# Index block: the sample tile first, its scores with the cached keys between the prompt's score steps, single PSUM banks

## The chip, the cores and the metric

The kernel runs on one core of a Trainium2 chip. The metric is the device time of one launch in microseconds (us); lower is better. Engines are TensorE (PE), VectorE (DVE), ScalarE (ACT), GpSimd (POOL) and the DMA queues that SyncE (SP) and POOL issue to.

## What is computed

The program is one inference step of a two-layer decoder for a prompt of 1024 tokens and a sample group of 8 x 8 = 64 tokens. The part that is changed is the lightning indexer at the start of each layer: it scores keys for each query, and the best 256 are kept later.

```
z = x @ w_in_l
qi = rope(a_qi.reshape(B, L, IDX_HEADS, IDX_DIM), pos) * (IDX_DIM ** -0.5)
ki = rope(a_ki[:, :, None, :], pos)[:, :, 0, :]
wi = a_w * (IDX_HEADS ** -0.5)
def index_scores(qi, ki, wi):
    dots = jnp.einsum('bthd,bsd->bths', qi.astype(F32), ki.astype(F32))
    return jnp.einsum('bth,bths->bts', wi.astype(F32), jax.nn.relu(dots))
```

A prompt query is scored with the prompt's keys up to itself. A sample query is scored with 2048 cached keys of its own batch entry, gathered through a page table, and with the 8 new keys. There are 8 heads of 32. Everything is in f32.

## The kernel before

Each of the two layers runs a chain of blocks; between two blocks all engines meet. The first is `index_block` (line 406), the second `mixer_block`, whose DVE begins at once with the top-k search (`find`, lines 318 and 322) over the scores that `index_block` left, and whose PE begins at once with the input projections (line 889).

`index_block` works on nine tiles of tokens: 0 to 7 are 128 prompt rows each, 8 is the 64 sample rows. Its parts, on each engine in program order:

- **Transposed input.** PE turns all nine tiles (line 478) and ACT and DVE copy them to SBUF.
- **Per tile t:** PE multiplies the tile by the index columns of the weights (line 523, eight matmuls of 296 columns, the "input group" below). ACT copies the result (lines 602, 603). DVE applies the rotary embedding (lines 680 to 689, "rope"). PE turns the roped rows (`turn`, line 489), one tile later, and ACT copies them (`qk`, line 581). The input group has two PSUM banks in turn (4 and 5), the turned rows two (6 and 7).
- **Score steps** (`score_steps`, line 394). Prompt tiles 2 to 7 have 2, 2, 4, 4, 4 and 4 steps: a step is 256 to 512 keys by four of the eight heads. PE makes four row-packed matmuls into four banks (`score`, line 508), ACT takes the relu of all four (`relu`, line 592, "score relu") into one of two buffers `r`, and DVE adds the heads up with their weights (`add`, lines 660 and 662). The steps of tile t-2 stand in the program behind the input group of tile t. The sample tile's own keys are one more step (`own_step`, line 512), just ahead of tile 7's four. Up to it all steps use banks 0 to 3; tile 7's alternate between banks 0 to 3 and 4 to 7.
- **Sample scores with the cached keys**, after all steps: eight pairs of matmuls (`sample_score`, line 550: two row tiles of 64 rows, 512 keys, into two banks), one relu over both (line 617), and two matmuls that sum over heads (`sample_sum`, line 559), with a last copy to the score tile `S` (line 619). They need the sample's queries spread out by DVE (16 copies, line 706) and the weights turned (lines 692, 535, 610).

POOL gathers the cached keys by 32 indirect DMAs (line 627) from the block's start; SP writes the block's input rows out (lines 452, 453), since `r` takes their place, and loads the mixer's first weights (line 462) when the last input group is done. Semaphores in the code order everything: `s_sr` counts score relus, `s_sp` score steps on PE, `s_zs`, `s_zr`, `s_zd` the sample's scores, relus and sums.

Of the kernel before, what the change touches and what calls it, by code (L numbers as in the profile page):

```python
# [31 lines left out]
P = 128  # L32
# [373 lines left out]


def index_block(e):
# [19 lines left out]
    own_step = next(n for n, x in enumerate(steps) if x[0] == NT - 1)  # L428
    of_tile = lambda t: [n for n, x in enumerate(steps) if x[0] == t]
    set_of = lambda n: (n - own_step) % 2 if n > own_step else 0  # L430
    added = [4 * (n + 1) + (4 if n >= own_step else 0) for n in range(len(steps))]
# [13 lines left out]
    with nc.Block() as block:  # L445
# [23 lines left out]
        def _(pe):  # L469

            for t in range(NT):
                R = rows(t)
                for half in range(2):
                    g = 2 * t + half
# [8 lines left out]
            def turn(t):  # L483
                R = rows(t)
                pe.wait_ge(s_ro, t + 1)
                if t >= 2:
                    pe.wait_ge(s_qk, t - 1)
                for n, src in enumerate((rr[0:R, t % 2, 0:128], rr[0:R, t % 2, 128:256], kr[0:R, t % 2, :])):
                    ins = pe.transpose(bank(6 + t % 2)[:, n * P:n * P + R], src, ident[0:R, 0:R])
                ins.then_inc(s_qp, 1)  # L490

            def score(n):
                t, _, a, b, g = steps[n]
                pe.wait_ge(s_qk, t + 1)
# [3 lines left out]
                if n == own_step + 1:  # L498
                    pe.wait_ge(s_zi, NT)
                    pe.wait_ge(s_qk, NT)  # L500
                    pe.wait_ge(s_ws, 1)
                before = [m for m in range(n) if set_of(m) == set_of(n)]
                if before:
                    pe.wait_ge(s_sr, before[-1] + 1)
                for h in range(4):
                    part, out = slice(32 * h, 32 * h + 32), bank(4 * set_of(n) + h)
# [9 lines left out]
            for t in range(NT):  # L516
                R = rows(t)
                pe.wait_ge(s_ta, t + 1)
                pe.wait_ge(s_td, t + 1)
                if t >= 2:  # L520
# [5 lines left out]
                if t:  # L526
                    turn(t - 1)
                for n in of_tile(t - 2):
                    score(n)
            turn(NT - 1)  # L530

            pe.wait_ge(s_wd, 1)
            pe.wait_ge(s_zi, NT - 1)
            for pair in range(4):
                ins = pe.transpose(bank(5)[:, pair * NS:(pair + 1) * NS], WD[0:NS, pair * P:(pair + 1) * P],
                                   ident[0:NS, 0:NS])
            ins.then_inc(s_wt, 1)
            for n in range(own_step, len(steps)):
                score(n)

            def sample_score(n):
                a, g = n // 2, n % 2
                if n == 0:
                    pe.wait_ge(s_qb, 1)
                    pe.wait_ge(s_kit, layer * (16 * 2 * NPG) + 16 * 2 * NPG)
                if n >= 2:
                    pe.wait_ge(s_zr, n - 1)
                for rr_ in range(2):
                    part = slice(64 * rr_, 64 * rr_ + 64)
                    ins = pe.matmul(bank(2 * (n % 2) + rr_), QB[part, g, :], kitc[part, g, 512 * a:512 * a + 512],  # L550
                                    start=True, stop=True)
                ins.then_inc(s_zs, 1)

            def sample_sum(n):
                a, g = n // 2, n % 2
                pe.wait_ge(s_zr, n + 1)
                for rr_ in range(2):
                    half = a // 2
                    ins = pe.matmul(bank(4 + a % 2)[64 * half:64 * half + 64, :], WS[:, 2 * g + rr_, :],
                                    rs[:, n % 2, 512 * rr_:512 * rr_ + 512],  # L560
                                    start=(g == 0 and rr_ == 0), stop=(g == 1 and rr_ == 1))
                ins.then_inc(s_zd, 1)

            pe.wait_ge(s_sr, len(steps))
            sample_score(0)
            for n in range(8):
                if n < 7:
                    sample_score(n + 1)
                sample_sum(n)

        @block.scalar
        def _(act):
            ch = chains(e, act, "act")
            for t in range(NT):
                act.wait_ge(s_tp, 2 * t + 1)
                act.copy(XT[:, 0:4, tcol(t)], bank((2 * t) % 4).rearrange("p (c n) -> p c n", c=4)[:, :, 0:rows(t)]
                         ).then_inc(s_ta, 1)

            def qk(t):
                act.wait_ge(s_qp, t + 1)  # L580
                act.copy(QKI[:, :, tcol(t)], bank(6 + t % 2, 384).rearrange("p (c n) -> p c n", c=3)[:, :, 0:rows(t)]
                         ).then_inc(s_qk, 1)

            def relu(n):
# [5 lines left out]
                if n >= 2:  # L590
                    act.wait_ge(s_sd, added[n - 2])
                act.activation(r[0:R, n % 2, 0:4 * w].rearrange("p (h s) -> p h s", h=4),
                               ps[0:R, 2048 * set_of(n):2048 * set_of(n) + 2048].rearrange(
                                   "p (h s) -> p h s", h=4)[:, :, 0:w], ACT.Relu).then_inc(s_sr, 1)

            for t in range(NT):
                R = rows(t)
                act.wait_ge(s_zp, t + 1)
                if t >= 2:
                    act.wait_ge(s_ro, t - 1)  # L600

                act.mul(w_idx[0:R, t, :], bank(4 + t % 2, 296)[0:R, 288:296], (ID * IH) ** -0.5)
                act.copy(zi[0:R, t % 2, 0:288], bank(4 + t % 2, 296)[0:R, 0:288]).then_inc(s_zi, 1)
                if t:
                    qk(t - 1)
                for n in of_tile(t - 2):
                    relu(n)
            qk(NT - 1)
            act.wait_ge(s_wt, 1)
            act.copy(WS.rearrange("p a s -> p (a s)"), bank(5, 4 * NS)).then_inc(s_ws, 1)  # L610
            for n in range(own_step, len(steps)):
                relu(n)
            for n in range(8):
                act.wait_ge(s_zs, n + 1)
                if n >= 2:
                    act.wait_ge(s_zd, n - 1)
                act.activation(rs[:, n % 2, :], ps[:, 1024 * (n % 2):1024 * (n % 2) + 1024], ACT.Relu).then_inc(s_zr, 1)
            act.wait_ge(s_zd, 8)
            act.copy(S[:, SOFF:SOFF + HALF], ps[:, 2048:3072]).then_inc(s_ss, 1)
# [2034 lines left out]
```

## Time and profile before

| | |
|---|---|
| time, median of 3 runs | 4244.15 us (4241.81 to 4248.46) |
| profiled execution: its time / its span | 4248.55 us / 4246.7 us |
| busy: PE, DVE, ACT, POOL | 3840.8 (90%), 2057.7 (48%), 978.3 (23%), 1171.1 (28%) |
| mean granted TensorE clock | 0.924 of 2.4 GHz |

The shares of the whole span tell little here: the program is a chain of blocks with different limits. The block that the change touches is read in stretches of its own, once per layer: from 25.8 to 163.6 us in the first and from 2129.7 to 2270.1 us in the second. In the profile an f32 matmul leaves two records, so x8 on PE is four matmuls.

### The profile page before, as it was taken

The numbers are of one execution on the slowest core, as the hardware profiler recorded it, in microseconds if no ns is written. First come the engines' busy times: TensorE is split into PE (matmuls) and PEld (weight loads), VectorE is DVE, ScalarE is ACT, GpSimd is POOL, SyncE is SP. The second block draws the span as 40 slices with busy tenths as digits, with TensorE's granted clock in tenths as the row PEclk, the third lists the DMA queues.
The fourth block names the chain that finished last, engine by engine and source line by source line (L and its number), as shares of the span: only waits on it lengthen the run. The fifth ranks groups of instructions, "written<-read, shape, count | busy, mean of one in ns | idle before, by whom it ended". The sixth has DMA issues, their size and how long they took to land. (4 is left out here: it accounts for less than half of the span.)

```text
span 4246.7 us, 50144 instructions
## 1 busy us (share of the span) xinstructions
PE 3840.8 (90%) x18986; PEld 2644.4 (62%) x18986; DVE 2057.7 (48%) x4149; ACT 978.3 (23%) x1930; POOL 1171.1 (28%) x1043
## 2 busy tenths in 40 slices
PE   6899977889897999999879999878898989999996
PEld 4344564444466988889643445644445578889985
DVE  5799564533044333333667994555221443333335
ACT  3201134420132221112231012344211221111222
POOL 3014672313023112122330155622130322122113
PEclk9899957989998999999979999579899989999998
DMA  3111002460211111111020110034602121111101
GB/s 141 41 44 39 14 1 86 160 220 21 79 40 60 49 50 40 40 40 43 6 96 26 41 45 6 1 135 149 202 0 80 40 80 40 40 40 40 56 33 42
DMA packets 143022, 254.97 MB, mean 60 GB/s; under 512 B 24577, under 2 KB 76162, under 8 KB 142594
## 3 DMA queue, kind: packets, MB, share of 16 engines
q1 hardware_dynamic: 130562, 215.00, 14.8%
q0 software_dynamic: 12288, 37.76, 2.6%
q8 instruction: 98, 1.61, 0.2%
q14 instruction: 74, 0.61, 0.0%
HBM read 231.31 MB, written 21.42 MB: 60 GB/s over the span
## 5 line engine op out<-in xcount | busy, mean ns | idle before, releaser
L2403 PE MATMUL ps<-ffn_parts 128*128 128x512 f32 (+1 forms) x3456 | 801.7, 391 | 7.4 <-DVE arena L2533 7.4
L2393 PE MATMUL ps<-ffn_parts 128*128 128x384 f32 (+1 forms) x4608 | 778.6, 329 | 23.0 <-POOL ffn_parts L2478 23.0
L2393 PEld LDWEIGHTS ps<-ffn_parts 128*128 128x128 f32 x4608 | 774.3, 189 | 28.2 <-POOL ffn_parts L2478 23.9
L2403 PEld LDWEIGHTS ps<-ffn_parts 128*128 128x128 f32 (+1 forms) x3456 | 623.4, 182 | 174.7 <-DVE arena L2533 24.3
L2533 DVE TENSOR_TENSOR arena<-arena,ps 128x1024 f32<-128x1024 f32 (+1 forms) x288 | 351.2, 1219 | 342.3 <-PE ps L2403 338.2
L889 PE MATMUL ps<-arena,arena_rest 128*128 128x512 f32 (+1 forms) x1152 | 379.5, 492 | 3.7 <-PEq L445 2.7
L2483 POOL TENSOR_TENSOR ffn_parts<-arena,ffn_parts 128x1024 fp32r<-128x1024 f32 x64 | 153.9, 2404 | 607.5 <-ACT ffn_parts L2437 607.5
L899 PE MATMUL ps<-arena_rest,arena 128*128 128x512 f32 (+3 forms) x864 | 318.7, 526 | 2.3 <-ACT arena_rest L1072 2.3
L889 PEld LDWEIGHTS ps<-arena,arena_rest 128*128 128x128 f32 x1152 | 191.7, 193 | 193.5 <-issue 192.1
L322 DVE TENSOR_SCALAR_CACHE_REDUCE arena_rest<-arena_rest,small 128x384 bf16<-128x384 f32 (+4 forms) x330 | 278.8, 875 | 2.1
L1941 PE MATMUL ps<-arena_rest,arena 128*128 128x512 f32 (+1 forms) x576 | 256.0, 604 | 20.7 <-DMA arena_rest<-in_w_out 20.7
L2525 DVE TENSOR_TENSOR arena<-arena 128x384 f32<-128x384 f32 (+1 forms) x96 | 77.1, 828 | 363.8 <-ACT arena L2456 363.8
L899 PEld LDWEIGHTS ps<-arena_rest,arena 128*128 128x128 f32 (+1 forms) x864 | 157.7, 185 | 142.3 <-issue 130.9
L1865 POOL TENSOR_TENSOR arena<-arena,arena_rest 128x1024 f32<-128x1024 f32 (+1 forms) x34 | 79.7, 2345 | 493.3 <-DVE arena L1857 493.3
L2437 ACT CAST ffn_parts<-arena 128x1024 fp32r<-128x1024 f32 x64 | 67.1, 1049 | 640.6 <-PE ps L2403 618.3
L1502 POOL DMA_INDIRECT arena_rest<-in_kv,kv_rows x128 | 135.4, 1058 | 277.4 <-PE ps L1616 239.7
L1941 PEld LDWEIGHTS ps<-arena_rest,arena 128*128 128x128 f32 (+1 forms) x576 | 106.9, 188 | 159.8 <-issue 137.1
L318 DVE TENSOR_SCALAR_CACHE_REDUCE arena_rest<-arena_rest,small 128x1088 bf16<-128x1088 f32 (+1 forms) x132 | 168.0, 1310 | 2.4
L949 PE MATMUL ps<-arena_rest 64*128 64x64 f32 (+2 forms) x1088 | 127.6, 405 | 45.4 <-POOLq L1263 23.7
L2478 POOL TENSOR_TENSOR ffn_parts<-arena,ffn_parts 128x512 fp32r<-128x512 f32 x64 | 82.2, 1295 | 305.9 <-ACT ffn_parts L2434 305.9
L2525 DVE TENSOR_TENSOR ffn_raw<-ffn_raw 128x384 f32<-128x384 f32 (+1 forms) x96 | 48.4, 532 | 241.9 <-ACT ffn_raw L2456 241.9
L2478 POOL TENSOR_TENSOR ffn_parts<-ffn_raw,ffn_parts 128x512 fp32r<-128x512 f32 x64 | 84.7, 1334 | 280.0 <-ACT ffn_parts L2434 280.0
(299 smaller groups left out, 4951.4 us busy)
## 6 DMA issues: line engine op xcount, KB each, us to landing
arena_rest<-in_kv SPq DMA_DIRECT2D x128, 256.0 KB
arena<-in_w_down SPq DMA_DIRECT2D x32, 1024.0 KB, 7.6
arena_rest<-in_w_in SPq DMA_DIRECT2D x10, 2048.0 KB, 8.1
ffn_raw<-in_w_up SPq DMA_DIRECT2D x16, 1024.0 KB, 5.9
arena<-in_w_up SPq DMA_DIRECT2D x16, 1024.0 KB, 5.9
out_y_prompt<-arena SPq DMA_DIRECT2D x3, 4096.0 KB, 15.9
arena<-out_y_prompt SPq DMA_DIRECT2D x2, 4096.0 KB, 24.8
arena_rest<-in_mem_kT SPq DMA_DIRECT2D x16, 512.0 KB, 7.1
```

What stands on the lines that cost most here:

```text
L318: ch.mark(dve.tensor_scalar(M16[:, moff:moff + w], S[:, off:off + w], thr[:, i:i + 1], None, op, ALU.add, accum_out=cnt[:, i:i + 1]))
L322: ch.mark(dve.tensor_scalar(M16[:, moff:moff + w], S[:, off:off + w], thr[:, i:i + 1], None, op, ALU.add, accum_out=cnt[:, i:i + 1]))
L889: ins = pe.matmul(ps[:, (f % 2) * 1536 + a:(f % 2) * 1536 + b], buf[:, k, c * P:(c + 1) * P], XT[:, k, a:b], start=(k == 0), stop=(k == KC ...
L899: ins = pe.matmul(bank(6 + u % 2, w)[0:R, :], XT[:, k, tcol(t)], buf[:, k, c0:c0 + w], start=(k == 0), stop=(k == KC - 1))
L949: ins = pe.matmul(second(ps[0:R, a:a + R], m), lhs[part, c, cols], second(rhs[part, c, cols], m), start=True, stop=True)
L1502: pool.indirect_dma_start(KV[b % 2][1][:, pg, :], None, i["kv"].rearrange("n p w -> (n p) w"), bass.IndirectOffsetOnAxis(ap=e["kvrow"][:, ...
L1941: ins = pe.matmul(bank(2 * (t % 2) + a)[0:R, :], YT[:, k, tcol(t)], WO[:, k, 512 * a:512 * a + 512], start=(k == 0), stop=(k == KC - 1))
L2393: ins = pe.matmul(bank(3 * c + b, y - x), w[:, k, :], h[:, k, x:y], start=(k == 0 and h is HH and w is WH), stop=(k == KC - 1 and w is WL))
L2403: ins = pe.matmul(bank(b0 + a)[0:R, :], u[:, c, tcol(t)], d[:, c, 512 * a:512 * a + 512], start=(c == 0 and u is UH and d is DH), stop=(c ...
L2478: pool.tensor_tensor(WL[:, ks, :], WU[n][:, ks, c * P:(c + 1) * P], WH[:, ks, :], ALU.subtract).then_inc(s_uh, 1)
L2483: pool.tensor_tensor(DL[:, c, :], WD[:, c, :], DH[:, c, :], ALU.subtract).then_inc(s_dl, 1)
L2533: dve.tensor_tensor(X[0:R, t, :], X[0:R, t, :], ps[0:R, b0:b0 + 1024], ALU.add).then_inc(s_ad, 1)
```

## The change

1. **The sample tile comes first.** `TILES` puts tile 8 ahead of tiles 0 to 7 in every loop; `j` is the place in that order. Its own-key step is step 0, the turning of its weights (DVE, PE, ACT) stands at place 1, the 16 spreading copies and the own-key adds on DVE at place 2.
2. **The cached-key scores are cut in 16 units** (one matmul of 64 rows by 512 keys, one relu, one summing matmul), all through bank 7, and stand behind score steps 9 to 20: on PE `score(n)`, then the sum of the unit before and the score of this one; on ACT the score relu of step n, then the unit's. Steps 14, 16 and 18 carry two units, and the last unit stands behind all steps. Sums gather in bank 6, and ACT copies each finished half out (`summed`).
3. **Single banks elsewhere:** the input group has bank 4 alone, turned rows bank 5, all score steps banks 0 to 3.

```diff
 def score_steps():
-    steps = []
+    steps = [(NT - 1, 0, 0, 2 * NS, 0)]
     for t, off, w in score_jobs():
-        if t == NT - 2:
-            steps.append((NT - 1, 0, 0, 2 * NS, 0))
...
-    set_of = lambda n: (n - own_step) % 2 if n > own_step else 0
+    TILES = [NT - 1] + list(range(NT - 1))
+    UNITS = [(a, g, rr_) for a in (0, 2, 1, 3) for g in range(2) for rr_ in range(2)]
+    units_behind, u = {n: [] for n in range(len(steps))}, 0
+    for n in range(9, len(steps)):
+        k = 2 if n in (14, 16, 18) else 1
+        units_behind[n] = list(range(u, u + k))
+        u += k
+    units_last = list(range(u, len(UNITS)))
...
             def score(n):
-                before = [m for m in range(n) if set_of(m) == set_of(n)]
-                if before:
-                    pe.wait_ge(s_sr, before[-1] + 1)
+                else:
+                    pe.wait_ge(s_sr, n)
...
+            def sample_score(u):
+                a, g, rr_ = UNITS[u]
+                if u == 0:
+                    pe.wait_ge(s_qb, 1)
+                    pe.wait_ge(s_kit, layer * (16 * 2 * NPG) + 16 * 2 * NPG)
+                else:
+                    pe.wait_ge(s_zr, u)
+                part = slice(64 * rr_, 64 * rr_ + 64)
+                pe.matmul(bank(7), QB[part, g, :], kitc[part, g, 512 * a:512 * a + 512],
+                          start=True, stop=True).then_inc(s_zs, 1)
+            def sample_sum(u):
+                pe.wait_ge(s_zr, u + 1)
...
+                pe.matmul(bank(6)[half:half + 64, :], WS[:, 2 * g + rr_, :], rs[:, u // 2 % 2, 512 * rr_:512 * rr_ + 512],
+                          start=(u % 4 == 0), stop=(u % 4 == 3), skip_group_check=True).then_inc(s_zd, 1)
+            def sample(u):
+                if u:
+                    sample_sum(u - 1)
+                sample_score(u)
...
-                if t >= 2:
-                    pe.wait_ge(s_zi, t - 1)
+                if j:
+                    pe.wait_ge(s_zi, j)
                 for k in range(KC):
-                    ins = pe.matmul(bank(4 + t % 2, 296)[0:R, :], XT[:, k, tcol(t)], wb[:, k, :],
+                    ins = pe.matmul(bank(4, 296)[0:R, :], XT[:, k, tcol(t)], wb[:, k, :],
...
-                for n in of_tile(t - 2):
+                for n in of_place(j - 2):
                     score(n)
+                    for u in units_behind[n]:
+                        sample(u)
...
+            def sample(u):
+                a, g, rr_ = UNITS[u]
+                act.wait_ge(s_zs, u + 1)
+                if u >= 4:
+                    act.wait_ge(s_zd, u - 3)
+                act.activation(rs[:, u // 2 % 2, 512 * rr_:512 * rr_ + 512], bank(7), ACT.Relu).then_inc(s_zr, 1)
+                if u % 4 == 1 and u > 4:
+                    summed(u // 4 - 1)
```

On PE the score steps of tile 5 and what follows stood so before (a row is a run of equal matmuls; line 523 is the input group, 489 `turn`, 508 a score step's four matmuls):

```order
L489 MATMUL ps<-cst,arena_rest 128x128 x3
L508 MATMUL ps<-arena_rest 128x384 x16
L523 MATMUL ps<-arena_rest,arena 64x296 x8
L489 MATMUL ps<-cst,arena_rest 128x128 x3
L508 MATMUL ps<-arena_rest 128x512 x8
L508 MATMUL ps<-arena_rest 128x384 x8
```

and stand so now (line 507 is `score`, 523 `sample_score`, 534 `sample_sum`, 493 `turn`):

```order
L493 MATMUL ps<-cst,arena_rest 128x128 x3
L507 MATMUL ps<-arena_rest 128x384 x4
L519 ISA
L523 MATMUL ps<-arena_rest 128x512
L507 MATMUL ps<-arena_rest 128x384 x4
L534 MATMUL ps<-arena,arena_rest 64x512
L523 MATMUL ps<-arena_rest 128x512
L507 MATMUL ps<-arena_rest 128x384 x4
L534 MATMUL ps<-arena,arena_rest 64x512
L523 MATMUL ps<-arena_rest 128x512
```

The sample's input group is gone from between the tiles, and from step 10 on two unit matmuls stand between two score calls (at step 9 one).

The end of the block on PE, before (550 and 559 are the paired scores and the sums, in eight rounds of which three show):

```order
L489 MATMUL ps<-cst,arena_rest 128x64 x3
L535 MATMUL ps<-cst,arena_rest 128x64 x4
L512 MATMUL ps<-arena_rest 64x64 x8
L508 MATMUL ps<-arena_rest 128x512 x16
L545 ISA
L550 MATMUL ps<-arena_rest 128x512 x4
L559 MATMUL ps<-arena,arena_rest 64x512 x2
L550 MATMUL ps<-arena_rest 128x512 x2
L559 MATMUL ps<-arena,arena_rest 64x512 x2
```

and now, from step 19 to the block's end:

```order
L507 MATMUL ps<-arena_rest 128x512 x4
L534 MATMUL ps<-arena,arena_rest 64x512
L523 MATMUL ps<-arena_rest 128x512
L507 MATMUL ps<-arena_rest 128x512 x4
L534 MATMUL ps<-arena,arena_rest 64x512
L523 MATMUL ps<-arena_rest 128x512
L534 MATMUL ps<-arena,arena_rest 64x512
L523 MATMUL ps<-arena_rest 128x512
L534 MATMUL ps<-arena,arena_rest 64x512
```

Behind the last score step two units are left where eight rounds stood.

On DVE, place 2 of the new order (the roped tile 1, then the 16 spreading copies of line 723, the own-key adds of lines 681 and 679, then the rope of tile 2):

```order
L708 COPY arena_rest<-arena_rest 128x128
L723 COPY arena_rest<-arena_rest 32x2x2x8 x16
L725 ISA
L681 TENSOR_SCALAR arena_rest<-arena,small 64x64
L679 SCALAR_TENSOR_TENSOR arena_rest<-arena,small,arena_rest 64x64 x7
L690 MEMSET arena_rest 64x64
L691 TENSOR_TENSOR arena_rest<-arena_rest,cst 64x64
L699 TENSOR_TENSOR arena_rest<-arena_rest,cst 128x288
```

Before, these copies and adds stood between the adds of tile 6 and those of tile 7.

## Rows read from the trace of the kernel before

**Rows 1.** Timeline, first layer's index block: landmarks (start us, us, engine line op; idle before <- releaser)

```profile
35.47 8.24 PE L523 MATMUL ps<-arena_rest,arena 128*128 128x296 f32 x32
...
56.92 0.93 PE L508 MATMUL ps<-arena_rest 32*128 32x384 f32 x8
...
90.56 1.45 ACT L592 ACTIVATE arena<-ps 128x1536 f32<-128x1536 f32 x1 [0.37 <-PE ps L508]
...
162.30 1.01 ACT L619 COPY arena_rest<-ps 128x1024 f32<-128x1024 f32 x1 [2.54 <-PE ps L559]
163.62 0.18 DVE L1301 TENSOR_SCALAR kidx_rows<-kidx_rows 128x32 int32<-128x32 int32 x1 [23.21 <-PEq L445]
```

**Rows 2.** Timeline, second layer: the same score relu and mixer start

```profile
2196.92 1.45 ACT L592 ACTIVATE arena<-ps 128x1536 f32<-128x1536 f32 x1 [0.36 <-PE ps L508]
...
2270.11 0.18 DVE L1301 TENSOR_SCALAR kidx_rows<-kidx_rows 128x32 int32<-128x32 int32 x1 [22.77 <-PEq L445]
```

**Rows 3.** Windows: from:to length, busy PE, PEld, DVE, ACT, POOL, then granted clock

```profile
73.70:82.50 8.80, 4.26 (x34) 1.75 (x33) 8.28 (x19) 4.54 (x5) 0.00 (x0) 0.71 0.01 2
82.50:89.50 7.00, 7.00 (x23) 4.93 (x19) 2.92 (x7) 1.18 (x3) 0.00 (x0) 0.63 0.00 1
89.50:115.70 26.20, 15.51 (x77) 5.94 (x75) 19.64 (x39) 12.63 (x13) 0.00 (x0) 0.73 0.26 84
...
143.00:163.00 20.00, 19.27 (x53) 5.10 (x52) 0.00 (x0) 6.83 (x7) 0.00 (x0) 1.00 0.00 1
163.60:430.00 266.40, 257.29 (x727) 122.19 (x728) 259.42 (x643) 26.53 (x53) 66.09 (x89) 0.99 0.13 44
```

**Rows 4.** Timeline, first layer: input group, turn, ACT's copy; sample's own work on PE and DVE

```profile
43.55 0.49 PE L489 MATMUL ps<-cst,arena_rest 128*128 128x128 f32 x3
...
43.82 0.39 ACT L603 COPY arena_rest<-ps 128x288 f32<-128x288 f32 x1
43.87 4.15 PE L523 MATMUL ps<-arena_rest,arena 128*128 128x296 f32 x16
...
119.23 0.73 PE L512 MATMUL ps<-arena_rest 32*64 32x64 f32 x16 [0.83 <-ACT arena_rest L581]
...
121.82 3.23 DVE L706 COPY arena_rest<-arena_rest 32x32 f32<-32x32 f32 x16
...
125.42 2.15 DVE L660 SCALAR_TENSOR_TENSOR arena_rest<-arena,small,arena_rest 64x64 f32<-64x64 f32 x7
```

**Rows 5.** Timeline, first layer: score calls that waited for the relu before; a 512-key relu

```profile
59.51 0.93 PE L508 MATMUL ps<-arena_rest 32*128 32x384 f32 x8 [1.66 <-ACT arena L592]
...
68.10 1.14 PE L508 MATMUL ps<-arena_rest 32*128 32x512 f32 x8 [2.09 <-ACT arena L592]
...
110.47 1.88 ACT L592 ACTIVATE arena<-ps 128x2048 f32<-128x2048 f32 x1 [2.29 <-PE ps L508]
```

**Rows 6.** Timeline, first layer: the sample's relu of 512 columns, scores and sums

```profile
120.05 0.59 ACT L592 ACTIVATE arena<-ps 64x512 f32<-64x512 f32 x1 [0.60 <-PE ps L512]
...
136.21 3.78 PE L550 MATMUL ps<-arena_rest 64*128 64x512 f32 x8 [4.43 <-ACT arena L592]
...
157.56 1.13 PE L550 MATMUL ps<-arena_rest 64*128 64x512 f32 x4
158.62 3.65 PE L559 MATMUL ps<-arena,arena_rest 128*64 128x512 f32 x8
```

**Rows 7.** Timeline, first layer: DVE adds of two steps, and of one 384-key pair

```profile
76.79 4.61 DVE L660 SCALAR_TENSOR_TENSOR arena_rest<-arena,small,arena_rest 128x384 f32<-128x384 f32 x7
...
134.54 5.54 DVE L660 SCALAR_TENSOR_TENSOR arena_rest<-arena,small,arena_rest 128x512 f32<-128x512 f32 x7
```

**Rows 8.** First layer: write-out of sample rows, last gather (timeline); landing (DMA issues)

```profile
27.44 1.48 SPq L453 DMA_DIRECT2D out_y_sample<-arena  x1
...
67.73 1.01 POOL L627 DMA_INDIRECT arena_rest<-in_kidxT,kidx_rows  x1 [0.30 <-issue]
...
out_y_sample<-arena SPq DMA_DIRECT2D x1, 256.0 KB, 18.9
```

More of the change, by code:

```diff
@@ L469, in _ @@
         def _(pe):
-            for t in range(NT):
+            for j, t in enumerate(TILES):
                 R = rows(t)
                 for half in range(2):
-                    g = 2 * t + half
+                    g = 2 * j + half
                     if g >= 4:
@@ L481, in _, with turn @@
             pe.wait_ge(s_w, 16)
[L483 to L489 removed]
+            def turn(j):
+                R = rows(TILES[j])
+                pe.wait_ge(s_ro, j + 1)
+                if j:
+                    pe.wait_ge(s_qk, j)
+                for n, src in enumerate((rr[0:R, j % 2, 0:128], rr[0:R, j % 2, 128:256], kr[0:R, j % 2, :])):
+                    ins = pe.transpose(bank(5)[:, n * P:n * P + R], src, ident[0:R, 0:R])
                 ins.then_inc(s_qp, 1)
@@ L524, in _ @@
                                     start=(k == 0), stop=(k == KC - 1))
                 ins.then_inc(s_zp, 1)
-                if t:
-                    turn(t - 1)
-                for n in of_tile(t - 2):
+                if j:
+                    turn(j - 1)
+                if j == 1:
+                    pe.wait_ge(s_wd, 1)
+                    for pair in range(4):
+                        ins = pe.transpose(bank(6)[:, pair * NS:(pair + 1) * NS], WD[0:NS, pair * P:(pair + 1) * P],
+                                           ident[0:NS, 0:NS])
+                    ins.then_inc(s_wt, 1)
@@ L541, in sample_score @@
[L541 to L569, printed above, removed]
+            for j in (NT - 2, NT - 1):
+                for n in of_place(j):
+                    score(n)
+                    for u in units_behind[n]:
+                        sample(u)
+            for u in units_last:
+                sample(u)
+            sample_sum(len(UNITS) - 1)
         @block.scalar
@@ L592, in relu @@
                 act.activation(r[0:R, n % 2, 0:4 * w].rearrange("p (h s) -> p h s", h=4),
-                               ps[0:R, 2048 * set_of(n):2048 * set_of(n) + 2048].rearrange(
-                                   "p (h s) -> p h s", h=4)[:, :, 0:w], ACT.Relu).then_inc(s_sr, 1)
-            for t in range(NT):
-                R = rows(t)
[L598 to L606, printed above, removed]
+                               ps[0:R, 0:2048].rearrange("p (h s) -> p h s", h=4)[:, :, 0:w], ACT.Relu
+                               ).then_inc(s_sr, 1)
@@ new lines, in relu, with summed @@
+                for u in units_behind[n]:
+                    sample(u)
+            def sample(u):
+                a, g, rr_ = UNITS[u]
+                act.wait_ge(s_zs, u + 1)
[4 more added lines that the diff above has]
+                    summed(u // 4 - 1)
+            def summed(m):
+                a = UNITS[4 * m][0]
+                half = slice(64 * (a // 2), 64 * (a // 2) + 64)
+                act.wait_ge(s_zd, 4 * m + 4)
+                act.copy(S[half, SOFF + 512 * (a % 2):SOFF + 512 * (a % 2) + 512], bank(6)[half, :]).then_inc(s_ss, 1)
@@ new lines, in _ @@
+            for j, t in enumerate(TILES):
+                R = rows(t)
+                act.wait_ge(s_zp, j + 1)
+                if j >= 2:
+                    act.wait_ge(s_ro, j - 1)
+                act.mul(w_idx[0:R, t, :], bank(4, 296)[0:R, 288:296], (ID * IH) ** -0.5)
+                act.copy(zi[0:R, j % 2, 0:288], bank(4, 296)[0:R, 0:288]).then_inc(s_zi, 1)
+                if j:
+                    qk(j - 1)
+                if j == 1:
+                    act.wait_ge(s_wt, 1)
+                    act.copy(WS.rearrange("p a s -> p (a s)"), bank(6, 4 * NS)).then_inc(s_ws, 1)
+                for n in of_place(j - 2):
@@ L607, in _ @@
                     relu(n)
             qk(NT - 1)
[L609 to L617, printed above, removed]
@@ L618, in _ @@
-            act.wait_ge(s_zd, 8)
-            act.copy(S[:, SOFF:SOFF + HALF], ps[:, 2048:3072]).then_inc(s_ss, 1)
+            for j in (NT - 2, NT - 1):
+                for n in of_place(j):
+                    relu(n)
+            for u in units_last:
+                sample(u)
+            summed(3)
             keep(e, ch, "act")
@@ L634, in _ @@
             ch = chains(e, dve, "dve")
-            for t in range(NT):
-                dve.wait_ge(s_tp, 2 * t + 2)
+            for j, t in enumerate(TILES):
+                dve.wait_ge(s_tp, 2 * j + 2)
                 dve.tensor_copy(XT[:, 4:8, tcol(t)],
-                                bank((2 * t + 1) % 4).rearrange("p (c n) -> p c n", c=4)[:, :, 0:rows(t)]
+                                bank((2 * j + 1) % 4).rearrange("p (c n) -> p c n", c=4)[:, :, 0:rows(t)]
                                 ).then_inc(s_td, 1)
```

91 lines of the change are left out of this document (43 added, 48 removed).

## The prediction

> **What bounds the kernel now.** I read the block's timeline first, for its landmarks, then windows of its stretches, then the rows of the parts that move.
>
> The tail shows at once. DVE's first mixer instruction starts at 163.62 us after 23.21 us of idling, so its last add ended at 140.41 [rows 1]; the second layer has 22.77 us of the same [rows 2]. In that tail PE and ACT score the sample against the cached keys while DVE has nothing. What follows starts only when the block ends, and it has no slack to take up a later or earlier start: from 163.6 to 430 us DVE is busy 259.42 of 266.40 us and PE 257.29 [rows 3]. So whatever the block's end gains or loses, I carry one to one to the kernel's end, twice (two layers).
>
> Ahead of the tail the steps of tiles 5 to 7 are limited by a loop of PE and ACT: with one set of banks a score call waits for the relu before it, 0.93 + 1.66 = 2.59 us per 384-key step and 1.14 + 2.09 = 3.23 us per 512-key step at the full clock [rows 5]. DVE needs less, about 5.54 plus one first product per two 512-key steps and 4.61 plus one per two 384-key steps, some 3.0 and 2.5 us a step [rows 7]. And the granted clock is low there: 0.73 from 89.5 to 115.7 us [rows 3], a mixture of the two levels, 2.4 and 1.2 GHz.
>
> **The front (cost).** The sample tile now precedes the first score step of tile 2, which stood at 56.92 us, 21.45 after the input groups began at 35.47 [rows 1]. Added ahead of it: one input group and one turn, 4.15 + 0.49 = 4.64 us; the turning of the sample's weights, four transposes, 0.65 by the three of a turn (0.49), and its own-key scores 0.73 [rows 4]. The single bank 4 makes each later group wait for ACT's copy: that copy runs 43.82 to 44.21, where the next group began at 43.87 [rows 4], so about 0.40 us with the semaphore, five times, 2.0 us. On DVE the 16 spreading copies (3.23) and own-key adds (2.15 and the first product) [rows 4] stand ahead of the rope of tile 2, which so comes about 6 us later. Its `turn` stands behind one more input group, 4.15 and that group's waits, and I put what is left of the 6 us at 0.8 on PE's path; then DVE catches up, since no prompt adds come before tile 2's. Sum 4.64 + 0.65 + 0.73 + 2.0 + 0.8 = 8.8, taken as **9.0 us later** per layer. The ends: 4.6 if the bank waits hide the small work, 13 if all of DVE's extra work showed.
>
> The waits that move ahead cost nothing as long as their cover holds. The own-key relu now waits at about 51 us (three groups and the small work behind 35.47) for the write-out of the block's input rows; the later of its two DMAs is issued at 27.44 and lands 18.9 us on, at 46 [rows 8]. If it came later, ACT would stand there with the copies of the next tiles behind it, one for one. The first unit waits on PE for the gathers; POOL issues the last at 67.73 [rows 8] and the unit comes near 100 us. SP issues the key write-out and the mixer's first weights some 10 us earlier than before, behind the same two waits, next to no other transfer; the mixer's PE did not wait for them before, so nothing is gained.
>
> **Tiles 2 to 4** use one set of banks before and after, and carry no units: as before, 9.0 us later. So the first score relu of tile 5 moves from 90.56 [rows 1] to 99.6.
>
> **From that relu to the block's end.** Before: 162.30 + 1.01 - 90.56 = 72.75 us [rows 1]. After, counted on the PE-ACT loop at 2.4 GHz:
>
> - A unit gives PE a sum and a score. Four sums take 3.65 us, so a sum 0.86 with its fill left out [rows 6]; a lone score streams the same 512 columns, so also 0.86. Pairs ran both row tiles in 1.13 [rows 6]; the units give that up. The 1.72 us of a unit stand beside the score relu, for which PE idled 2.09 or 1.66 us [rows 5]: hidden, but for 0.06 us at 384 keys. The unit's relu (0.59 for as many columns [rows 6]) runs while the next score call does. A step with one unit thus costs what it costs without.
> - Steps 9 to 12: 3 x 2.59 = 7.8. Step 12 to 13: 1.45 + 1.34 with the `turn` of tile 7 squeezed in, 3.1 (1.34 is the 3.23 less the relu's 1.88 [rows 5]). Single steps 13, 17, 19: 3 x 3.23 = 9.7. Step 15: 2.6.
> - Double steps 14, 16, 18: here PE needs the first unit's relu before the second's score. Between two score relus lie the relu (1.88, at 16 1.45), the unit's relu 0.59 and a handover of 0.1, a sum and a score 1.72, the next score call and its handover 1.34 or 1.13: 5.4, 5.4 (with a `summed` copy of about 0.6 half hidden) and 5.6, 16.3 in all, 2.3 us each above a single.
> - To here 39.4. Then the last relu 1.88, the relu of unit 14 0.6, sum 0.93, score 1.13 + 0.13, relu 0.59, sum 1.1, handovers 0.2 and a last copy 0.6: 7.1. **46.5 us.**
>
> DVE is not the bound in it: the adds of tiles 5 to 7 are 5.0 + 5.0 + 6.0 + 5.0 + 6.0 + 6.0 = 33 us with three causal adds, under 39.4 + 1.88, and its last add then ends about 2 us ahead of ACT's last copy. That is the 23 us of idling gone.
>
> **Sum.** 9.0 + 46.5 - 72.75 = -17.2 us in the first layer. In the second the relu is at 2196.92 and the mixer starts at 2270.11 [rows 2], 0.3 after ACT's end as in the first: 72.9, so -17.4. Together -34.6. The profiled execution took 4248.55 us, 4.4 above the median; the sum on it gives 4213.9, on the median 4244.15 - 34.6, and I forecast **4210**. With the front at its ends the two layers give 4201 or 4218.
>
> **What the single banks cost** is in this sum: the doubles' 2.3 us each, and tile 7's steps, which ran at DVE's 3.0 us with two sets and loop at 3.23 with one [rows 5, 7]; together some 8 us a layer.
>
> **Rivals.**
>
> - *The clock stays at 1.2 GHz (slower).* In tile 4's steps, one score call of about 0.9 us every 2.6, the granted clock fell (0.71 from 73.7 to 82.5 us), and it was still low for most of the tile-7 input group, 0.63 from 82.5 to 89.5 [rows 3]. At 1.2 GHz two score pairs take 3.78 us [rows 6], so a lone matmul near 1.71. Then PE is the bound: 1.71 + 3.42 = 5.1 per 512-key step, 4.7 per 384, 9.3 to 9.7 per double; 68 + 13.4 for the tail = 82 in place of 46.5, +18.3 us a layer: 4281. The kernel is slower from the point where more than about half of the steps run at 1.2. Against it: PE would have no gap in single steps, and where it had none the clock rose: within the input group at 82.5 to 89.5 (0.63 is a mixture), and after the first pairs at 136.21, with 1.00 from 143 to 163, where sums and pairs alternate with ACT much as the units do [rows 3, 6]. For it: no row shows lone 64-row scores at length, and tile 4's steps show how soon it falls.
> - *The clock falls in the double steps only.* PE waits about 1.3 us in each for the two relus (1.14 + 0.13 + 1.88 + 0.59 + 0.1 from the score call's start, less 0.86 + 1.72 of work). At 1.2 GHz the three cost 28.7 in place of 16.3: -5 us a layer, 4234. The Trainium skill, "TensorE: Matmul & The Clock Gate", section A second HAM failure mode: psum-queue depth-cycling, tells of just this: short idles between groups that cycle through PSUM banks made the clock swing in one kernel. The trace agrees from 89.5 to 115.7 us of before (0.73), and disagrees from 143 to 163 (1.00).
> - *The clock holds through tile 4 too*, by another timing of it: the input group of tile 7 then takes 4.15 us [rows 4] in place of 6.5, which is the 7.00 from 82.5 on [rows 3] less its turn: -2.4 a layer, 4205.
> - *The end of the block does not count*: something in the mixer waits for another thing. Against it, rows 3's busy DVE and PE. 4244.
>
> **How the numbers follow.** Forecast 0.66, clock high through tile 4 0.08, doubles slow 0.12, all slow 0.09, no effect 0.05. A measurement of this kernel can tell about 0.2%, 8.5 us, from no change. Faster takes the first two and most of the third (4234 lies just beyond 4235.7): 0.84; the rest of it and the last make same 0.07; slower 0.09. The range, 4196 to 4238, takes in the front's ends (the lower of them with the high clock 4196) and the slow doubles; left out are the all-slow case and no effect, 0.14, and some strays.
>
> **What would show it.** Right: the first score call of tile 2 near 66 us, the first score relu of tile 5 near 99.6, DVE's first mixer instruction near 146.5 after idling of about 2 us in place of 23.21; granted clock near 1.00 from there to the end of the block; double steps of 5.4 us, single ones of 2.6 and 3.2. Wrong: unit matmuls of 1.7 us in tiles 6 and 7 with clocks near 0.5; ACT idle ahead of the own-key relu; the mixer not as much shorter as the block.

## The result and the profile after

The changed kernel takes **4221.4 us** (median of 5 runs, 4218.4 to 4227.8) where the kernel before takes 4244.15: ratio 0.9947, interval 0.9933 to 0.9962. It is faster by 22.7 us; 34 were forecast. The profiled execution took 4227.81 us (span 4226.0, before 4246.7), with a mean granted clock of 0.932.

The first layer's index block on its timeline, the rows that answer to [rows 1] (line 549 is the input group, 493 `turn`, 507 a score call, 596 the score relu, 615 `summed`):

```profile
37.01 4.20 PE L549 MATMUL ps<-arena_rest,arena 128*64 128x296 f32 x16
41.85 4.22 PE L549 MATMUL ps<-arena_rest,arena 128*128 128x296 f32 x16 [0.64 <-ACT arena_rest L624]
...
56.52 4.23 PE L549 MATMUL ps<-arena_rest,arena 128*128 128x296 f32 x16 [0.32 <-ACT arena_rest L624]
...
62.38 0.55 PE L493 MATMUL ps<-cst,arena_rest 128*128 128x128 f32 x3 [1.64 <-DVE arena_rest L708]
...
67.18 0.93 PE L507 MATMUL ps<-arena_rest 32*128 32x384 f32 x8
...
102.02 1.45 ACT L596 ACTIVATE arena<-ps 128x1536 f32<-128x1536 f32 x1 [0.36 <-PE ps L507]
...
144.36 1.88 ACT L596 ACTIVATE arena<-ps 128x2048 f32<-128x2048 f32 x1
...
150.96 0.58 ACT L615 COPY arena_rest<-ps 64x512 f32<-64x512 f32 x1 [1.16 <-PE ps L534]
151.84 0.18 DVE L1321 TENSOR_SCALAR kidx_rows<-kidx_rows 128x32 int32<-128x32 int32 x1 [2.14 <-PEq L449]
```

DVE's idling ahead of the mixer fell from 23.21 to 2.14 us, and the mixer starts 11.8 us earlier. The first tile-5 relu stands 11.5 later, and from it to the mixer lie 49.82 us where 73.06 lay [rows 1]. The second layer, as [rows 2]:

```profile
2199.89 1.45 ACT L596 ACTIVATE arena<-ps 128x1536 f32<-128x1536 f32 x1 [0.36 <-PE ps L507]
...
2249.72 0.18 DVE L1321 TENSOR_SCALAR kidx_rows<-kidx_rows 128x32 int32<-128x32 int32 x1 [2.15 <-PEq L449]
```

49.83 us again, for 73.19 before. Windows of the changed kernel, first layer (columns as in [rows 3]: length, busy PE, PEld, DVE, ACT, POOL, granted clock, DMA share, GB/s):

```profile
70.00:92.00 22.00, 17.01 (x78) 9.69 (x74) 16.44 (x34) 9.54 (x11) 0.00 (x0) 0.84 0.02 4
92.00:101.00 9.00, 7.37 (x35) 4.89 (x35) 6.52 (x14) 2.50 (x5) 0.00 (x0) 0.81 0.00 0
102.00:114.00 12.00, 11.39 (x50) 3.32 (x51) 10.07 (x20) 8.45 (x9) 0.00 (x0) 1.00 0.59 188
114.00:150.00 36.00, 32.34 (x105) 8.15 (x106) 23.37 (x36) 22.83 (x23) 0.00 (x0) 1.00 0.00 0
152.00:420.00 268.00, 258.29 (x726) 122.36 (x726) 261.05 (x643) 26.15 (x52) 66.01 (x88) 0.98 0.13 44
```

The granted clock is 1.00 wherever units stand between score steps; before it was 0.73 from 89.5 to 115.7 us, in the steps of tiles 5 and 6 [rows 3]. The mixer looks as it did: DVE is busy 261.05 of 268.00 us.

How a step runs now, around score relus 11 and 14 (523 is a unit's score, 534 its sum, 607 its relu, PEld the weight load):

```profile
106.53 0.93 PE L507 MATMUL ps<-arena_rest 32*128 32x384 f32 x8
106.64 0.60 ACT L607 ACTIVATE arena<-ps 128x512 f32<-128x512 f32 x1 [0.58 <-PE ps L523]
...
107.39 1.07 PE L534 MATMUL ps<-arena,arena_rest 128*64 128x512 f32 x2
107.53 1.45 ACT L596 ACTIVATE arena<-ps 128x1536 f32<-128x1536 f32 x1 [0.29 <-PE ps L507]
108.39 0.29 PEld L523 LDWEIGHTS ps<-arena_rest 64*128 64x128 f32 x2 [0.81 <-issue]
108.39 1.12 PE L523 MATMUL ps<-arena_rest 64*128 64x512 f32 x2
...
109.44 0.93 PE L507 MATMUL ps<-arena_rest 32*128 32x384 f32 x8
...
119.94 1.07 PE L534 MATMUL ps<-arena,arena_rest 128*64 128x512 f32 x2 [0.69 <-ACT arena L607]
120.95 1.12 PE L523 MATMUL ps<-arena_rest 64*128 64x512 f32 x2
122.00 0.93 PE L507 MATMUL ps<-arena_rest 32*128 32x384 f32 x8
```

PE starts a score call at 106.53, the sum 0.86 later, the score 1.00 after that, the next score call 1.05 after that: 2.91 us without a gap, where the loop of PE and ACT took 2.59. In the double step PE waits 0.69 us for a unit's relu, and the sum and the score take 2.06 again.

### The profile page after: what moved, and what is told of

Its sections match the earlier page's. It is cut to its first block and busy times, and to the rows that moved or that the text cites. A ratio compares the mean times of both kernels' runs of the same rounds, so it can differ in the third digit from the quotient of the medians.

```text
span 4226.0 us, 50180 instructions
## 1 busy us (share of the span) xinstructions
PE 3846.3 (91%) x18986; PEld 2643.1 (63%) x18986; DVE 2060.2 (49%) x4149; ACT 983.0 (23%) x1952; POOL 1171.5 (28%) x1043
```

## The experiments

Twelve kernels ran. All are edits of the changed kernel. "From the tile-5 relu" is the time from the first score relu of tile 5 to the mixer's start, 49.8 us in the changed kernel. A ratio is to the kernel before as it ran beside that experiment; its medians lie between 4244.2 us (beside the changed kernel) and 4250.0, so a difference of a few us between kernels that did not run side by side tells nothing. The block is counted from its first transpose to the mixer's start.

**1. The order without the interleave.** No units between the steps; the paired scores of the kernel before follow all steps. The sample tile stays first, and banks 0 to 3 serve all steps.

```diff
-    for n in range(9, len(steps)):
-        k = 2 if n in (14, 16, 18) else 1
+    for n in range(0):
+        k = 1
...
```

> The changed kernel with the sample tile still first and the single banks for the tiles, but no units between the steps: the eight paired rounds of the kernel before stand behind all steps again (sums in banks 6 and 7). Theory A (the gain is made by the units between the steps, which hide under the score relus and hold the clock): the front stays, first score relu of tile 5 near 102 us as in the changed kernel; the steps of tiles 5 to 7 fall back to a mixed clock (0.6 to 0.8) and take about 37 us to the last score relu; from there the 29 us of the kernel before. The block lasts about 142 us in the first layer, against 137.8 before and 125.6 changed; time 4245 to 4258. Rival B (the order of the tiles makes the gain, and the units only move work): the block is as short as changed, 126 to 128 us, time near 4222.

Measured: 4258.1 us, ratio 1.002 (1.001 to 1.0029). Its steps and its end:

```profile
100.09 1.45 ACT L623 ACTIVATE arena<-ps 128x1536 f32<-128x1536 f32 x1 [0.36 <-PE ps L507]
...
107.58 1.66 PE L507 MATMUL ps<-arena_rest 32*128 32x384 f32 x8 [1.65 <-ACT arena L623]
...
115.06 2.09 PE L507 MATMUL ps<-arena_rest 32*128 32x512 f32 x8 [2.08 <-ACT arena L623]
...
140.50 1.88 ACT L623 ACTIVATE arena<-ps 128x2048 f32<-128x2048 f32 x1 [2.29 <-PE ps L507]
...
169.79 0.18 DVE L1352 TENSOR_SCALAR kidx_rows<-kidx_rows 128x32 int32<-128x32 int32 x1 [23.94 <-PEq L449]
```

```profile
100.00:140.00 40.00, 20.52 (x95) 6.28 (x91) 29.15 (x50) 18.46 (x12) 0.00 (x0) 0.55 0.18 57
```

The order and the single banks alone cost time. The DVE idling is back at 23.94 us, and the clock is at 0.55 in the same steps, so the gain is the interleave's. From the first tile-5 relu to the last score relu lie 40.41 us here and 42.34 in the changed kernel, which has fourteen units in between: at the full clock the steps and these units together take 1.9 us more than the bare steps at the low one, and what follows the last score relu falls from 29.29 to 7.48 us.

**2. No doubles.** One unit behind each of steps 9 to 20, four at the end (`k = 1`).

> The changed kernel with one unit behind each of the steps 9 to 20 and the last four behind all steps: no double steps. Theory A: a second unit in a step costs about 2.7 us (5.73, 6.06 and 5.95 us between score relus where single ones took 2.9 to 3.2), a unit in the tail 2.81 us, so nothing changes: block 125 to 126.5 us, time 4219 to 4224. Rival: the doubles also hold DVE up and cost more than the tail does; then the block is 2 to 5 us shorter in each layer, time 4211 to 4217.

Measured: 4220.9 (0.9935, 0.9918 to 0.9951), no change. From the tile-5 relu 49.9 us. From the last score relu to the mixer it is 15.92 us for 7.48 in the changed kernel, with three units more: 2.81 a unit, against the 2.7 to 2.9 by which a double is longer than a single. So a unit in a double step costs what it costs in the tail.

**3. Units earlier, behind steps 5 to 20 singly.**

```diff
-    for n in range(9, len(steps)):
-        k = 2 if n in (14, 16, 18) else 1
+    for n in range(5, len(steps)):
+        k = 1
```

> The changed kernel with one unit behind each of the steps 5 to 20: no double steps, and nothing left behind the last step but the 16th unit's own chain. Theory A (steps of tile 4 can hide a unit as those of tile 5 do, and with units the clock holds there): the three doubles' 2.7 us each go, tile 4's steps stay near 2.6 to 2.9 us, the input group of tile 7 takes 4.2 in place of 5.3 to 6.6 us; block about 116 to 118 us in the first layer in place of 125.6; time 4199 to 4206. Rival B (256-key steps are too short for a unit of 2.05 us on PE, and DVE is behind there, so what goes from the doubles comes back in tile 4): block 121 to 125, time 4211 to 4221.

Measured: **4200.5** (4200.0 to 4201.9; 0.9893, 0.9877 to 0.9908), the best of all, as theory A said. The first layer's block, from 26.20 us in both kernels, is 115.34 us where the changed kernel has 125.64:

```profile
85.74 1.45 ACT L596 ACTIVATE arena<-ps 128x1536 f32<-128x1536 f32 x1 [0.36 <-PE ps L507]
...
95.87 4.25 PE L549 MATMUL ps<-arena_rest,arena 128*128 128x296 f32 x16
...
101.37 1.45 ACT L596 ACTIVATE arena<-ps 128x1536 f32<-128x1536 f32 x1 [0.36 <-PE ps L507]
...
139.44 0.58 ACT L615 COPY arena_rest<-ps 64x512 f32<-64x512 f32 x1 [1.16 <-PE ps L534]
141.54 0.18 DVE L1321 TENSOR_SCALAR kidx_rows<-kidx_rows 128x32 int32<-128x32 int32 x1 [0.54 <-PEq L449]
```

```profile
85.00:100.00 15.00, 14.31 (x63) 5.92 (x60) 10.46 (x23) 7.60 (x9) 0.00 (x0) 1.00 0.01 2
```

Tile 4's four steps, 2.6 to 2.8 us apart, take four units; from its first relu to tile 5's lie 15.6 us in both layers, where the changed kernel has 13.8 and 15.7 without them. The doubles are gone, and tile 7's input group takes 4.25 us, at the full clock, where the changed kernel needs 5.26.

**4. Earlier still, behind steps 3 to 18.**

> The changed kernel with one unit behind each of the steps 3 to 18, nothing behind 19 and 20 and nothing left over. Theory A: as with units from step 5 on, and the last two steps have no unit to wait for: the tail behind the last score relu is DVE's add alone (about 5.5 us in place of 7.2) and the clock may fall in the last two steps (3.2 to 4.2 us each); block 114 to 117 us, time 4196 to 4204. Rival B: the gathers of the cached keys are not in when step 3 is reached (the last is issued at 68 us, step 3 comes near 77), PE stands there with the next input groups behind it, and the block is no shorter than with units from step 5.

Measured: 4208.9 (0.9915, 0.9902 to 0.9929), 8 us above experiment 3. The interval between score relus 4 and 5 is 7.44 us in both layers (7.07 and 6.42 in experiment 3), so tile 3's units lengthen the front; PE does not stand for the gathers there, as rival B had it, since relus 3 and 4 are 3.22 us apart. The blocks are 116.28 and 118.69 us (115.34 and 117.06 in experiment 3), which makes 2.6 of the 7.5 us between the two profiled executions. The rest lies outside the blocks, and its cause is open.

**5. The unit's score over 128 rows** (`QB[:, g, :]` and all rows of `kitc`). The two row halves are then summed into one score: that part of the result is altered.

> The changed kernel with each unit's score matmul over all 128 rows in place of 64 (the two row halves are added into one score; this part of the result is altered), all else the same. A lone unit matmul took 1.00 to 1.05 us from its start to the next one's, where I had put 0.86. Theory A: the extra 0.14 to 0.19 us is the change between 64-row and other tile shapes in the array: sum to score falls from 1.00 to about 0.86, 384-key steps with a unit from 2.92 to about 2.75, block 1.5 to 3 us shorter. Rival B: it is paid wherever one f32 matmul of one line follows that of another, whatever the rows: steps stay at 2.9, block within 0.7 us of the changed kernel's 125.6.

Measured: 4221.0 (0.9936, 0.992 to 0.9953). The spacings 1.05 and 1.00 and the 2.92 stay, as rival B said. The 64 rows aren't the cause.

**6. The spreading copies one place later** (`j == 3` for `j == 2` on DVE).

> The changed kernel with the 16 spreading copies on DVE at place 3 in place of 2, behind the rope of tile 2 and not ahead of it. Theory A (these copies held up the turn of tile 2: PE stood still before it, and the input group at place 5 began at 62.77 us, some 1.5 us late): that group begins 1.3 to 1.7 us earlier, the block is 1.3 to 1.7 us shorter in each layer, time 4217 to 4219. Rival B (bank 4 and the turn's own bank set the front, DVE only seems to): no change, block 125.6, time 4221.

Measured: 4221.65 (0.994, 0.9924 to 0.9957), no change. Tile 2's first score did come earlier (28.86 us behind the first input group in both layers, for 30.17 and 29.85), but the input groups of tiles 5 to 7 together took 1.2 and 1.3 us longer (tile 7's 6.64 in place of 5.26 in the first layer).

**7. One wait fewer.** The unit's score drops its `wait_ge(s_zr, u)`, which the sum ahead of it already implies.

> The changed kernel; on PE the unit's score no longer waits for the relu of the unit before, since the sum just ahead of it in the same queue already waits for that relu. In the changed kernel a sum and the score behind it start 1.00 us apart and that score and the next score call 1.05, where 512 columns stream in 0.86. Theory A (the extra 0.15 to 0.2 us of a lone matmul comes from a wait at the head of the matmul that follows, whose weights then are loaded late): sum to score falls from 1.00 to about 0.86, 384-key steps from 2.92 to about 2.78, the block by 1 to 2 us per layer, total about 4218 to 4220. Rival B (it belongs to the matmul itself or to the change of banks, not to the wait): 1.00 and 2.92 stay, total within 3 us of the changed kernel's 4221.

Measured: 4223.4 (0.994, 0.9926 to 0.9953). Spacings 1.00, 1.05 and steps of 2.92 as before: a semaphore wait that is already met isn't the cause.

**8. One sum of four.**

```diff
             def sample_sum(u):
+                if u % 4 < 3:
+                    return
...
```

> The changed kernel without three of every four summing matmuls (so the sample's scores with the cached keys hold one of four terms: that part of the result is altered). It frees about 1.0 us of PE per unit and changes nothing on ACT. Theory A (steps of 384 keys with a unit are bound by PE: score call 0.86, sum 1.00, score 1.05 = 2.92): they fall to 2.59, the loop of PE and ACT; the double steps lose the sum between the two scores, about 1.0 us each; the tail loses one sum; single 512-key steps stay at 3.23, since there the sum lay beside the relu. Together 1.2 + 2 to 3 + 1 = 4 to 5 us per layer, total 4211 to 4214. Rival B (the steps are bound by ACT's two relus and their handovers): the 384-key steps stay at 2.92, the doubles hardly move, total 4219 to 4222. Rival C (the units' matmuls keep the granted clock up): with less work on PE it falls below 1.00 between 100 and 150 us, and score calls take longer: total at or above 4221.

Measured: **4233.8** (0.9965, 0.9952 to 0.9979): 12 us slower than the changed kernel, with a quarter of its sums; its fastest run (4230.2) is slower than the slowest of the changed kernel (4227.8). Up to step 12 the 384-key steps take 2.58 us, as theory A said. Then, at the double step 14, PE waits 1.42 us for a unit's relu (here line 609), and what follows runs at half speed to the end of the block, in both layers:

```profile
113.76 1.12 PE L523 MATMUL ps<-arena_rest 64*128 64x512 f32 x2
...
116.30 2.07 PE L523 MATMUL ps<-arena_rest 64*128 64x512 f32 x2 [1.42 <-ACT arena L609]
118.30 1.66 PE L507 MATMUL ps<-arena_rest 32*128 32x384 f32 x8
```

Its windows:

```profile
110.00:115.00 5.00, 4.85 (x22) 1.12 (x14) 4.46 (x8) 3.77 (x4) 0.00 (x0) 1.00 0.04 12
115.00:120.00 5.00, 3.70 (x11) 1.12 (x11) 3.43 (x5) 2.30 (x4) 0.00 (x0) 0.63 0.00 0
120.00:125.00 5.00, 5.00 (x12) 1.19 (x12) 2.28 (x4) 3.42 (x3) 0.00 (x0) 0.50 0.00 0
...
145.00:150.00 5.00, 4.91 (x15) 1.54 (x12) 2.74 (x4) 3.59 (x4) 0.00 (x0) 0.50 0.02 3
```

From the tile-5 relu 57.5 and 57.4 us. Theory A holds as long as the clock is high, and C decides the time.

**9. Experiment 3 with the copies at place 3.**

> The best version so far (units singly behind steps 5 to 20, 4200.5 us) with the 16 spreading copies on DVE one place later, at place 3. Theory A (with the units begun at step 5 the front has become the longer part, and the copies at place 2 delay the rope of tile 2, about 3.2 us of DVE work): tile 2's first score comes about 2 us earlier and so does the block's end, total about 4196. Rival B (as in the run where the copies were moved in the changed kernel, another wait is as late, or the first unit then waits for the copies): total within 3 us of 4200.5.

Measured: 4203.2 (4200.3 to 4206.5; 0.9894, 0.9878 to 0.9909), no change, as rival B said.

**10 and 11. Two banks again for the early input groups** (4 and 7 in turn up to place 6), in the changed kernel and in experiment 3.

```diff
+    IN_BANK = [4, 7, 4, 7, 4, 7, 4, 4, 4]
...
-                    ins = pe.matmul(bank(4, 296)[0:R, :], XT[:, k, tcol(t)], wb[:, k, :],
+                    ins = pe.matmul(bank(IN_BANK[j], 296)[0:R, :], XT[:, k, tcol(t)], wb[:, k, :],
...
```

> The changed kernel with two PSUM banks in turn again for the input groups of the first seven places (banks 4 and 7; bank 7 is free until the first unit, which now also waits for its last copy). Theory A (the term of the forecast: each group waits about 0.40 us for ACT's copy of the group before, 2.0 us in all ahead of tile 2): the stretch from the first input group to tile 2's first score falls from 30.17 us to about 28.2, the block by as much, total about 4217. Rival B (in the changed kernel PE then waits 1.64 us at the turn of tile 2 for DVE's rope, which stands behind the 16 copies and the own-key adds: a wait for ACT ahead of it is hidden by that one): the stretch falls by under 1 us, total within 3 us of 4221.

> The same two banks in the best version so far (units singly behind steps 5 to 20, 4200.5 us). Theory A: about 2 us per layer earlier, total about 4196.5. Rival B: within 3 us of 4200.5, since there too the turn of tile 2 waits for DVE.

Measured: 4221.0 (0.9937, 0.9924 to 0.9951) and 4206.1 (4205.4 to 4209.4; 0.9901, 0.9886 to 0.9916). In the changed kernel so edited, the stretch to tile 2's first score fell by 0.75 us in the first layer and rose in the second (31.1 for 29.9). PE waits longer for DVE's rope at the turn of tile 2 (line 494 there; 1.64 in the changed kernel):

```profile
60.67 0.55 PE L494 MATMUL ps<-cst,arena_rest 128*128 128x128 f32 x3 [2.23 <-DVE arena_rest L710]
```

The first came out within what can be told from no change; the second is 5 us slower than experiment 3, which neither theory gave. Its blocks are no longer (115.47 and 116.67 us, for 115.34 and 117.06), so the difference lies outside them, and the two ratios' intervals overlap.

**12. Score and sum on one tile of the array.**

```diff
-                part = slice(64 * rr_, 64 * rr_ + 64)
-                pe.matmul(bank(7), QB[part, g, :], kitc[part, g, 512 * a:512 * a + 512],
+                M = 64 if u else 128
+                pe.matmul(bank(7)[0:M, :], QB[:, g, 0:M], kitc[:, g, 512 * a:512 * a + 512],
```

> The changed kernel with the unit's score over 128 rows and, from the second unit on, 64 columns of queries (so from there both row halves are summed into one score for half of the columns and the rest is stale: that part of the result is altered). A score and the sum ahead of it then use the same 128 by 64 tile of the array in units 1 to 3 and 8 to 11; in the other units the sum writes the upper half. Theory A (the 0.15 to 0.2 us by which a lone matmul exceeds its streaming is its fill, which the next one does not cover when it uses another tile): sum to score falls from 1.00 to about 0.87 us in units 1 to 3 and 8 to 11 and stays near 1.00 in 4 to 7; 384-key steps with a unit take about 2.79 us. Rival B (the tile has no part in it: two matmuls that follow a semaphore wait or change the bank never overlap): 1.00 and 2.92 everywhere. The total is within 3 us of 4221 by either.

Measured: 4210.35 (4208.4 to 4214.1; 0.991, 0.9894 to 0.9927), 11 us below the changed kernel where either theory gave no change. From the tile-5 relu 45.7 and 45.1 us. A 384-key step, and below it a step whose sum writes the upper half:

```profile
104.31 1.07 PE L534 MATMUL ps<-arena,arena_rest 128*64 128x512 f32 x2
...
104.79 0.14 PEld L523 LDWEIGHTS ps<-arena_rest 128*64 128x64 f32 x1 [0.29 <-issue]
105.22 1.02 PE L523 MATMUL ps<-arena_rest 128*64 128x512 f32 x2
...
106.17 0.93 PE L507 MATMUL ps<-arena_rest 32*128 32x384 f32 x8
...
118.93 0.64 PE L534 MATMUL ps<-arena,arena_rest 128*64 128x512 f32 x1 [1.47 <-ACT arena L607]
...
120.79 0.64 PE L534 MATMUL ps<-arena,arena_rest 128*64 128x512 f32 x1
...
120.80 0.64 PE L523 MATMUL ps<-arena_rest 128*64 128x512 f32 x1
```

On the same tile the score's weights load while the sum runs (104.79), and sum to score is 0.91 in place of 1.00, score to score call 0.95 in place of 1.05; the step takes 2.72. Theory A's number comes out near there, but not its reason. For units 4 to 7 (and 12 to 14), whose sums write the upper half, both theories were wrong: score and sum are on different tiles of one shape, 128 by 64, start 0.01 us apart and run side by side. So a change of tile by itself costs nothing here. What fits the extra is the change of the tile's shape, from the sum's 128 by 64 to the score's 64 by 128 (128 by 128 in experiment 5), or the score's 64 weight columns in place of 128, which came with it; the runs don't separate the two. Why the score call, whose shape differs as before, comes 0.10 sooner too isn't separated either.

## Why the prediction was right, and what it mis-sized

The sign, the mechanism and the range held; the size was 11 us too large. Its signs in the first layer came late by 1.2 us (first score call of tile 2, 67.18), 2.4 (tile-5 relu, 102.02) and 5.3 (DVE's first mixer instruction, 151.84).

- **The tail becomes beside-work: right.** DVE idles 2.14 us ahead of the mixer; about 2 was forecast. Experiment 1 shows that nothing else in the change pays.
- **The clock: right from the tile-5 relu on** (1.00). The rival of a clock that falls in the doubles is not far off: without three sums of four it happens in both layers, and the clock doesn't come back before the block ends. The Trainium skill, "TensorE: Matmul & The Clock Gate", section A second HAM failure mode: psum-queue depth-cycling, has short idles between groups of matmuls swing the clock in one kernel. The changed kernel's doubles disagree (waits of 0.69 us at 1.00); experiment 8 agrees that it falls, and shows it staying at 0.50 through windows in which PE is busy 4.91 to 5.00 of 5 us. The length of one wait doesn't decide it: in experiment 12 PE waits 1.47 us (at 118.93), longer than the 1.42 of experiment 8, and the clock stays at 1.00, as the window below shows. Behind a second such wait, at the end of the first layer's block, it falls to 0.59 from 145 to 146 us; in the second layer it does not fall.

```profile
120.00:125.00 5.00, 3.81 (x25) 0.98 (x24) 3.78 (x7) 4.03 (x5) 0.00 (x0) 1.00 0.00 0
```

- **The front of 9.0: right on average, and partly by luck.** To tile 2's first score it is 30.17 against 21.45 us, 8.7 more, for a sum of 8.8. But the waits for ACT's copy that show ahead of it are 0.64 and 0.32 us, where the sum had 2.0 for the single bank (two banks gave back 0.75 in one layer and nothing in the other), and DVE's rope, put at 0.8, shows as 1.64: the two misses partly cancel. From the block's start the first tile-5 relu comes at 75.82 and 76.93 us (64.70 and 67.19 before): 11.1 and 9.7 later. Over six kernels that differ little ahead of it (the changed one and experiments 2, 5, 6, 7 and 10) it lies between 73.3 and 76.9, mean 75.0, or 9.1 later than before. Part of the scatter comes with the input groups of tiles 5 to 7, which still meet a lowered clock (0.84 and 0.81 in the windows above; tile 7's takes 5.22 to 6.85 us in these profiles, where 4.15 is the full-clock time [rows 4]).
- **"A step with one unit thus costs what it costs without" failed for 384 keys.** The term was a sum and a score at 0.86 us each. They take 1.00 and 1.05, so PE, not the loop of PE and ACT, sets those steps: 2.92 for 2.59, and 3.60 for 3.1 at the turn of tile 7. The 512-key steps have room for it and stay at 3.22. The doubles hold one sum and one score on the path: 5.73, 6.06 and 5.95 us, 17.7 for 16.3. Together +3.0 us a layer: 49.8 us where 46.5 and the 0.3 to the mixer were forecast. The warning stood in [rows 6]: the pair at 157.56 is followed 1.06 us later by the sums, though it streams for 0.86. The 0.86 came from four sums in a row, on one tile; experiments 5 and 7 rule out the row count and the met wait, and experiment 12 ties about 0.1 us to the tile's shape or the score's columns. The rest wasn't separated. The Trainium skill, same page, section Single matmul latency, has a lone bf16 matmul at the full clock take a constant of 166 ns beside its columns; added to 0.86 that is an estimate of 1.03, which is near the 1.00 and 1.05.
- **One to one to the end: not refuted, not sharp.** The two blocks are 25.7 us shorter in the profiled executions, the span 20.7. What lies outside the blocks was 3968.6 us before and 3973.6 after, and between 3964.1 and 3973.9 in all profiles of this study, in no order by kernel. Of the forecast's 34.6 us, 13.9 are missing between the profiled executions: 6.0 for the steps, 2.9 for the front as it fell there, and 5.0 outside the blocks, within this scatter.
- **What the single banks cost: not tested by itself.** The forecast had tile 7's steps at DVE's 3.0 us with two sets of banks and at 3.23 with one. Before, with two sets, its last two score relus came 3.31 and 3.22 us behind the one ahead of each, waiting for DVE; with one set a single step takes 3.22 now, so in these steps no cost shows.

```profile
130.98 1.88 ACT L592 ACTIVATE arena<-ps 128x2048 f32<-128x2048 f32 x1 [1.44 <-DVE arena_rest L660]
...
134.20 1.88 ACT L592 ACTIVATE arena<-ps 128x2048 f32<-128x2048 f32 x1 [1.34 <-DVE arena_rest L660]
```

## What to carry to other kernels

Work moved into another engine's gaps is priced by the spacing of such instructions when they stand alone between unlike ones, not by their mean in a row of like ones; look for one row in which the switch already happens. On an engine whose clock falls when it idles, as PE's does here, filling gaps pays twice (experiment 1) and taking work away can cost: here fewer matmuls made the kernel 12 us slower. And in this kernel a filler was best put where PE idled at a low clock (tile 4's steps: experiment 3 is 21 us faster) before it was doubled up anywhere; starting two steps earlier still gained nothing more (experiment 4).

## What the runs showed of the hardware that was not expected

- Two matmuls of one queue, a sum into partitions 64 to 127 of one bank and a score into partitions 0 to 63 of another, both on 128 by 64 tiles, started 0.01 us apart and ran together (experiment 12); the first double step fell from 5.73 to 4.42 us.
- A lone f32 matmul of 512 columns takes 0.91 us to the next on the same 128 by 64 tile (experiment 12), and 1.00 to 1.05 to one on a tile of another shape (the changed kernel, where the score also has 128 weight columns and not 64).
- In experiment 8 the clock stayed at 0.50 from 120 to 150 us while PE was busy 4.27 to 5.00 of every 5 us; the changed kernel held 1.00 through the same stretch, busy 3.62 to 5.00 of every 5. What decides between the two isn't settled by these runs.

```profile
145.00:150.00 5.00, 3.62 (x8) 0.93 (x8) 4.16 (x7) 2.43 (x3) 0.00 (x0) 1.00 0.00 0
```
